# A streaming encoder step on one core: ten pairs for eleven between retrievals, longer runs for the activations, 112 down tiles in three passes

## The reference

```python
m = _mixer(_rmsnorm(x, norm1), ...)        # convolution and retention branches
x = x + m
x = x + _peer(_rmsnorm(x, norm2), wq, sk, u_tab, v_tab)
y = _rmsnorm(x, final_g)

# _peer, for each block of 128 tokens hb
q = (hb @ w_q).reshape(128, 8, 2, 128)
s = einsum('thpd,pkd->thpk', q, sk)                 # 8 heads, 2 sides, 128 keys
sv, si = top_k(s, 16)
cand = sv[:, :, 0, :, None] + sv[:, :, 1, None, :]  # 16 x 16 sums
ts, tp = top_k(cand, 16)                            # 16 experts per head
e = take_along_axis(cidx, tp, -1)                   # numbers in 0..16383
g = softmax(ts)
a = gelu(einsum('thkd,td->thk', u_tab[e], hb))
out = einsum('thkd,thk->td', v_tab[e], g * a)
```

## Time and profile before

| | us |
|---|---|
| median of 3 runs | 2256.77 (2254.47 to 2258.5) |
| the profiled execution | 2255.25 |
| its span, first to last instruction | 2253.4 |
| PE busy | 2175.2 (97%) |
| DVE busy | 1721.3 (76%) |
| POOL busy | 862.4 (38%) |
| ACT busy | 580.5 (26%) |

### The profile page before, as it was taken

One profiled execution on the slowest core, in us unless ns is written; L12 is line 12 of the kernel. 1 busy time (PEld: TensorE's weight loads), 2 busy tenths in 40 slices (PEclk: granted clock), 3 DMA queues, 4 the chain that ended last, 5 costly groups with the idle time before them and its releaser, 6 DMA issues.

```text
span 2253.4 us, 30667 instructions
## 1 busy us (share of the span) xinstructions
PE 2175.2 (97%) x10425; PEld 1683.0 (75%) x10425; DVE 1721.3 (76%) x3228; ACT 580.5 (26%) x1143; POOL 862.4 (38%) x606
## 2 busy tenths in 40 slices
PE   5999999999999999999999999999969999999998
PEld 5988989999998975655565565677737777777774
DVE  3576576676765277988979979999949888888885
ACT  3212223122222111211221211233314333333332
POOL 4322122123342005584684775311244444444430
PEclk9999999999999999999999999999989999999999
DMA  4999889999972459999999999888899999999992
GB/s 163 306 309 315 289 302 310 324 315 312 330 247 108 157 186 365 342 406 412 376 412 412 376 412 413 303 280 279 288 373 395 408 399 385 398 403 383 397 382 82
DMA packets 326439, 735.40 MB, mean 326 GB/s; under 512 B 30368, under 2 KB 179616, under 8 KB 326304
## 3 DMA queue, kind: packets, MB, share of 16 engines
q1 hardware_dynamic: 202080, 439.67, 54.5%
q0 software_dynamic: 73728, 268.47, 30.5%
q10 hardware_dynamic: 50496, 25.59, 3.8%
HBM read 604.04 MB, written 129.57 MB: 326 GB/s over the span
## 4 chain that ended last, share of the span: by engine, by line
PE 57%; DVE 14%; issue 13%; POOL 8%; DMA 7%; SPq 1%; ACT 1%; ACTq 0%; POOLq 0%; DVEq 0%
PE ps L1804 6%; PE ps L1805 6%; PE ps L1806 6%; PE ps L1751 6%; PE ps L1711 6%; PE ps L1812 5%; POOL b L680 5%; PE ps L1517 4%; PE ps L1516 4%; PE ps L1515 4%; PE ps L1766 3%; DVE b L1393 3%; DMA b<-in_peer_v,b 3%; POOL b L645 2%; DMA b<-in_u_t 2%
## 5 line engine op out<-in xcount | busy, mean ns | idle before, releaser
L1751 PE MATMUL ps<-b,b 128*128 128x384 f32 x2048 | 667.0, 487 | 0.0
L680 POOL DMA_INDIRECT b<-u_rows,b x256 | 363.9, 1421 | 743.3 <-DVE b L1376 543.4
L1751 PEld LDWEIGHTS ps<-b,b 128*128 128x128 f32 x2048 | 387.6, 190 | 264.1 <-issue 1.2
L645 POOL TENSOR_TENSOR b<-b,b 128x1024 fp32r<-128x1024 f32 x80 | 196.3, 2457 | 465.1 <-ACT b L693 460.6
L1515 PE MATMUL ps<-b,b 128*128 128x320 f32 x1152 | 364.5, 316 | 1.6 <-issue 1.6
L1393 DVE SCALAR_TENSOR_TENSOR b<-b,b,b 128x1024 f32<-128x1024 f32 x256 | 331.1, 1293 | 34.9 <-issue 16.9
L1517 PE MATMUL ps<-b,b 128*128 128x320 f32 x1152 | 357.1, 310 | 0.0
L1516 PE MATMUL ps<-b,b 128*128 128x320 f32 x1152 | 357.0, 310 | 0.0
L1376 DVE CUSTOM_DVE_ANT_0 b<-b,b 128x1024 f32<-128x1024 f32 x256 | 312.7, 1222 | 30.4 <-DMA b<-u_rows,b 24.4
L680 POOL DMA_INDIRECT b<-in_peer_v,b x256 | 289.3, 1130 | 91.5 <-issue 77.6
L1033 DVE STREAM_TRANSPOSE b<-b 128x1024 f32<-128x1024 f32 x128 | 157.6, 1240 | 166.2 <-DMA b<-in_u_t 161.3
(11 more groups left out here) (164 smaller groups left out, 2656.9 us busy)
## 6 DMA issues: line engine op xcount, KB each, us to landing
b<-in_u_t SPq DMA_DIRECT2D x256, 512.0 KB, 5.7
u_rows<-b SPq DMA_DIRECT2D x512, 128.0 KB, 4.2
b<-in_peer_v SPq DMA_DIRECT2D x128, 512.0 KB
b<-in_w_in SPq DMA_DIRECT2D x72, 512.0 KB
b<-in_wq SPq DMA_DIRECT2D x48, 512.0 KB
acts<-b SPq DMA_DIRECT2D x128, 192.0 KB
gates<-b ACTq DMA_DIRECT2D x12, 2048.0 KB
b<-gates SPq DMA_DIRECT2D x32, 768.0 KB
```

The costliest lines, as they stand in the source:

```text
L645: nc.gpsimd.tensor_tensor(lo[u][:, :], raw[:, u, :], hi[u][:, :].bitcast(F32), ALU.subtract).then_inc(lo_ready, 1)
L680: nc.gpsimd.indirect_dma_start(slots[n % SLOTS][:, :], None, u_rows if kind == "u" else v_rows, bass.IndirectOffsetOnAxis(ap=row_id[:, r_ ...
L1751: last = nc.tensor.matmul(ps[:, e % 4, 0:TD], w[:, k * P:(k + 1) * P], h2[:, k, SD:T], start=(k == 0), stop=(k == KT - 1))
```

## The change

In the order of the diff:

- `BEFORE_DOWNS` goes from five to six and `GAP` from eleven to ten. So each of three gaps has one pair less, one more stands before the downs, and 48 pairs instead of 46 are left for the down stage. `EXP_AT`, `SCORES_AT`, `PICKT_AT` and `GATE_AT` move up by one, two and three up products for the second, third and fourth retrieval with gaps before them; the scatters run in up products 96 to 119, and eight up products follow them instead of five. The slope of `pair_at` is 27.6.
- `three(e)` is true for seven of eight tiles, 112 in all, and no longer excludes the last four; there the tiles 124 to 126 are done in three passes, with the waits for their parts before the first token tile. `down_three` can end a sum.
- `acts` in memory is laid out by group, partition, tile: a group's load has one run of 6 KB for a partition instead of four of 1.5 KB. The stores stay one tile each.
- `fin_y`, `junk` and `fin_g` move onto the buffers of gates and activations (`al`, `gr`), and the load of `final_g` waits for the last product with gates alone.

```diff
--- before.py
+++ after.py
@@ -58,19 +58,19 @@
 BESIDE = 2
 AHEAD = 2
 BESIDE_HOTS = 8
-BEFORE_DOWNS = 5
+BEFORE_DOWNS = 6
 LINES = 4
 EXP_FIRST = -13
-EXP_AT = {1: 7, 2: 36, 3: 64, 4: 93}
-SCORES_AT = {2: 6, 3: 45, 4: 73}
-PICKT_AT = {2: 41, 3: 69, 4: 98}
-GATE_AT = 99
+EXP_AT = {1: 7, 2: 35, 3: 62, 4: 90}
+SCORES_AT = {2: 6, 3: 44, 4: 71}
+PICKT_AT = {2: 40, 3: 67, 4: 95}
+GATE_AT = 96
 GATE_ENDS = GATE_AT + TD // (2 * BLK)
 INSIDE = 9
 RETRIEVAL_AT = -7.6
 DOWN_RING = 2 * GROUP
 HALVES = 4
-GAP = 11
+GAP = 10
 CYCLE = INSIDE + GAP
 HOTS = 4
 EARLY = 4
@@ -89,7 +89,7 @@
         i = b - NPAIR_R
         return GATE_AT + 3 * i if i < BESIDE_HOTS else GATE_ENDS - 2 + i - BESIDE_HOTS
     turn, i = b // CYCLE, b % CYCLE
-    e = RETRIEVAL_AT + 28.6 * turn + (0.5 + 2.0 * i if i < INSIDE else 17.3 + 0.97 * (i - INSIDE))
+    e = RETRIEVAL_AT + 27.6 * turn + (0.5 + 2.0 * i if i < INSIDE else 17.3 + 0.97 * (i - INSIDE))
     return math.floor(e)
 
 
@@ -99,7 +99,7 @@
 
 def three(e):
 
-    return e < NKEY - GROUP and e % 6 != 5
+    return e % 8 != 7
 
 
 THREES = [e for e in range(NKEY) if three(e)]
@@ -339,25 +339,25 @@
 
 
         e = [z_from]
+        f = [z_from]
         al = take(e, [P, 2, GROUP, TD], F32)
         gr = take(e, [P, 2, NB, GROUP, GT], F32)
         p32 = take(e, [P, GROUP, TD], F32)
         p_hi = take(e, [P, GROUP, TD], F32R)
         p_lo = take(e, [P, GROUP, TD], F32R)
-        f = [e[0]]
         v_hi = [take(e, [P, D], F32R) for _ in range(HALVES)]
         v_lo = [take(e, [P, D], F32R) for _ in range(HALVES - 1)] + [at(h_from + 16384, [P, D], F32R)]
         v_more = [at(h_from + 4096 * i, [P, D], F32) for i in range(GROUP)]
         fin_y = take(f, [P, 2, D], F32)
         junk = take(f, [P, D], F32)
         fin_g = take(f, [P, D], F32)
-        assert f[0] <= e[0]
+        assert f[0] <= z_from + 16 * GROUP * TD
         assert e[0] <= top - 16384
 
         ps = ctx.enter_context(nc.psum_tensor("ps", [P, 8, 512], F32))
 
         gates = nc.dram_tensor("gates", [NE_GROUPS, P, NB, GROUP * GT], F32).ap()
-        acts = nc.dram_tensor("acts", [NKEY, P, TD], F32).ap()
+        acts = nc.dram_tensor("acts", [NE_GROUPS, P, GROUP, TD], F32).ap()
 
 
         loaded = [sem(f"raw_loaded{u}") for u in range(GROUP)]
@@ -580,7 +580,7 @@
 
             def acts_out(e):
                 sp.wait_ge(evac, A_U + e + 1)
-                sp.dma_start(tile_of(acts, e), spill[:, e % 2, :]).then_inc(a_stored[e % 2], 16)
+                sp.dma_start(acts[e // GROUP, :, e % GROUP, :], spill[:, e % 2, :]).then_inc(a_stored[e % 2], 16)
 
             for i in range(3 * A_WQ):
                 plain_in(i, io["wq"][i % A_WQ, :, :])
@@ -598,8 +598,8 @@
                     sp.wait_ge(a_stored[i], 16 * (GROUP // 2) * (g + 1))
                 src = gates[g, :, :, :]
                 sp.dma_start(gr[:, g % 2, :, :, :].rearrange("p b k t -> p b (k t)"), src).then_inc(g_loaded[g % 2], 16)
-                src = acts[g * GROUP:(g + 1) * GROUP, :, :].rearrange("k p t -> p k t")
-                sp.dma_start(al[:, g % 2, :, :], src).then_inc(al_loaded[g % 2], 16)
+                src = acts[g, :, :, :].rearrange("p k t -> p (k t)")
+                sp.dma_start(al[:, g % 2, :, :].rearrange("p k t -> p (k t)"), src).then_inc(al_loaded[g % 2], 16)
 
             def down_in(e):
                 if e < GROUP:
@@ -626,8 +626,7 @@
                     for u in range(GROUP):
                         down_in((g + 1) * GROUP + u)
 
-            sp.wait_ge(a_used, A_V + NKEY - GROUP)
-            sp.wait_ge(row_done, ROWS)
+            sp.wait_ge(p_ready, NKEY)
             sp.dma_start(fin_g[:, :], io["final_g"]).then_inc(fin_loaded, 16)
             for tt in range(TT):
                 sp.wait_ge(y_ready, tt + 1)
@@ -1796,6 +1795,10 @@
                 pe.wait_ge(v_loaded[e % DOWN_RING], 16 * (e // DOWN_RING + 1))
                 pe.wait_ge(p_ready, e + 1)
 
+            def split_in(e):
+                pe.wait_ge(v_split, SPLIT[e] + 1)
+                pe.wait_ge(p_split, SPLIT[e] + 1)
+
             def down_three(e, i):
                 u, n = e % GROUP, SPLIT[e] % HALVES
                 tok = slice(i * P, (i + 1) * P)
@@ -1803,7 +1806,7 @@
                     out, cols = ps[:, 2 + 2 * i + dh, :], slice(dh * 512, (dh + 1) * 512)
                     nc.tensor.matmul(out, p_hi[:, u, tok], v_hi[n][:, cols], start=(e == 0), stop=False)
                     nc.tensor.matmul(out, p_hi[:, u, tok], v_lo[n][:, cols], start=False, stop=False)
-                    last = nc.tensor.matmul(out, p_lo[:, u, tok], v_hi[n][:, cols], start=False, stop=False)
+                    last = nc.tensor.matmul(out, p_lo[:, u, tok], v_hi[n][:, cols], start=False, stop=(e == NKEY - 1))
                 return last
 
             def down(e, i):
@@ -1816,8 +1819,7 @@
             for e in range(NKEY - GROUP):
                 down_tile_in(e)
                 if three(e):
-                    pe.wait_ge(v_split, SPLIT[e] + 1)
-                    pe.wait_ge(p_split, SPLIT[e] + 1)
+                    split_in(e)
                 for i in range(ND):
                     last = down_three(e, i) if three(e) else down(e, i)
                 last.then_inc(a_used, 1)
@@ -1825,7 +1827,9 @@
                 for e in range(NKEY - GROUP, NKEY):
                     if i == 0:
                         down_tile_in(e)
-                    last = down(e, i)
+                    if i == 0 and three(e):
+                        split_in(e)
+                    last = down_three(e, i) if three(e) else down(e, i)
                 last.then_inc(sums_done, 1)
```

## The result

The changed kernel takes 2234.2 us (median of 4 runs, 2232.64 to 2235.69) where the kernel before takes 2255.62 beside it; the ratio is 0.9903, 95% interval 0.9889 to 0.9916, so 21.9 us less. The forecast was 2235.6 against 2256.77, 21.2 less. The profiled execution has a span of 2232.5 us; 2232.2 was forecast.

A forecast was written before the change was run, and what follows sets the result against it. PE, busy 2175 of 2253 us, was taken as the bound, with gaps bound by DMA. Gains of 7.7 + 5.1 + 8.4 = 21.2 us gave a span of 2232.2, or 2235.6 us in median terms; range 2225 to 2248.

The forecast's parts named there:

- A pair costs what DMA makes it cost, 23.2 us for three: Gaps between retrievals: dropping each gap's last pair frees DVE of 9.2, 7.15 and 6.85 us, DMA waiting included.
- the second rival: Up stage: a dropped pair saves only DVE's 4.7 us, the stage loses 1.3, total 2244.6 us; chance 0.13.
- The up stage, 7.7 us: Up products to end of scatters: pick waits nearly vanish, 0.2 us left, so the stage ends 7.7 us sooner.
- A gate write of 46 us, a gap of 17.4, 5.1 us: Before the downs: extra traffic lengthens the last gate write, yet PE's gap falls from 22.45 to 17.4, gaining 5.1 us.
- the first rival: Before the downs: the gate write is not prolonged, the gap falls to 7.0, total 2225 us; chance 0.17.
- My estimate from it, some 46 us: Last gate write: alternating its 512-byte runs with 4 KB gathers would keep it some 46 us if traffic lasts.
- Runs of 6 KB, nothing: Group loads of activations: 128 longer runs instead of 512 are worth zero, under 1 us at most.
- Eight tiles more in three passes, 8.4 us: Down products: eight more tiles at 4.10 us instead of 5.15 save 8.4 us if PE stays the bound.
- DVE's cover: Down stage: DVE's extra splits and pairs cost nothing, 38 us of its waiting for PE stays.
- DMA as the narrow cover: Down stage: tiles ask 403 GB/s against a seen ceiling of 410; costs nothing, with 2% of cover.
- The tail, nothing: After the last product: up to 1 us could appear, taken as zero; tail unchanged at 10 us.
- the third and fourth rivals: Down stage short of DMA: at 395 GB/s 2246 us, chance 0.10; at 380 GB/s 2268 us, chance 0.04.

The follow-up runs named there:

- moves_alone: Changed kernel's moved order constants and slope, but gaps of eleven pairs and five pairs before the downs again; ratio 0.9972, span 2244.2 us.
- bd0: Changed kernel with no pair between the scatters and the downs instead of six, 54 in the down stage; ratio 0.9912, span 2232.1 us.
- gap9: Changed kernel taken one step further: gaps of nine pairs, nine pairs before the downs, scatters from up product 93; ratio 0.9928, span 2232.0 us.
- acts_rows: Changed kernel with activations in memory as before, loaded in runs of 1.5 KB; ratio 0.9924, span 2237.4 us.
- threes_back: Changed kernel with 104 down tiles in three passes again, every sixth and the last four in plain fp32; ratio 0.9948, span 2240.9 us.
- bd4: Changed kernel with four pairs before the downs instead of six, 50 in the down stage; ratio 0.9885, span 2220.1 us.
- sp_order: Changed kernel with three more down tiles and activation writes ahead of the first group's load in SP's queue; ratio 0.9939, span 2241.9 us.

## Why the prediction was right, step by step

The sum was 21.2 us off the span, and 20.9 came. That it is so close is partly luck: the stages that the change touches gave 6.0 + 5.4 + 8.5 = 19.9, and 1.05 came from an earlier start of the up products. By its terms, in the profiles of the two kernels:

- *A pair costs what DMA makes it cost, 23.2 us for three.* Right: 22.6 us at the third retrieval, 21.5 counted from the first up product. 14.1, the second rival's price, is out.
- *The up stage, 7.7 us.* 6.0: from the first up product to the end of the scatters it went from 742.2 to 720.7, of which three products sooner are 15.5. The waits for picks stayed at 2.2 us instead of 0.2: at the third pick PE arrived 23.0 us sooner and not 22.1, DVE 22.6 and not 23.2. In absolute time the scatters ended at 1620.4, 22.6 sooner, as if the term had been 7.1; but 1.05 of this lies ahead of the up products and is chance. moves_alone shows that the moves pay nothing without the pairs. That the pairs need the moves is not shown: by the prediction's own working the waits of the picks would go with the pairs alone, and the moves are what shortens the gap; that kernel was not run.
- *A gate write of 46 us, a gap of 17.4, 5.1 us.* 45.6, 17.1 and 5.4. The choice was made against the optimistic end (a gap of 7.0, the first rival), and here the reading of full engines decided it. The plain sum of bytes, some 5 us for each 2.1 MB beside the write, holds while the gathers run dry before the write ends. "2.1 MB that need 5 us alone" were 7.2 us from issue to last packet in bd0. The Trainium skill's taking of turns, packet by packet, as cited in the prediction (DMA: Bandwidth & Descriptors, Queues, rings and completion order), is borne out by the packets of the queues, 659 of the write beside 657 of the gathers. My estimate from it, some 46 us, left out SP's queue and fails at gap9's 60.3; that it came near the measured 45.6 is luck.
- *Runs of 6 KB, nothing.* Borne out by road and down stage of acts_rows, in the profile; the interval of its runs is wider than the claim.
- *Eight tiles more in three passes, 8.4 us.* 8.5 between the two kernels and 8.4 in threes_back, both up to the end of the span. Up to the end of the last product it is 7.6 (552.0 to 544.4), and 0.9 lies in the tail. The products alone fell short because the stretch at half the clock behind the gap held 13 products instead of 7, at 0.2 us each. DVE's cover was worked out as 38 us left; the waits for PE that remain are 46.3.
- *DMA as the narrow cover.* 403 GB/s asked, 410 seen as the ceiling. It held, with windows of 49 to 92 us at 400 to 414. The true edge is 414: bd4 stands on it without loss, bd0 beyond it.
- *The tail, nothing.* DVE's last sums no longer wait for PE, and begin within 0.1 us of its end, though the load of final_g, 4.6 us, has come into the chain. From the last product to the end it is 9.1 us instead of 10.0; why is open.

So the third and fourth rivals, a down stage short of bytes, did not come. The nearest to them is bd0, which asks for more than the ceiling gives: their kind of sum, 1.80 MB at 414 GB/s for a tile against 4.23 us, gives 15 us there, and 9.2 came.

## What to carry to other kernels

When a wait ends on a transfer, ask what else the DMA engines carry until it lands: while they are full, each byte that is moved beside it delays it at the full rate, up to the time that its own turns take, and starting it sooner among more traffic gives that back (gap9 started the write 18 us sooner, won one in the profile and none in the runs). Short packets make a transfer weak among long ones: 512 bytes beside 4 KB got a twelfth of the bytes. And before you read a queue's release as a landing, see what else that queue had before it (bd0). Fill the stage that has PE as its bound with the DMA work up to the measured ceiling, and no further, and keep it away from the transfer that PE waits for. A step moved in one engine's order pays only as far as the engines that feed it come sooner too.

## What the hardware showed that I had not expected

Loads, stores and gathers together ran at 413 to 414 GB/s for 400 us on end in bd4, above the 358 that the Trainium skill (DMA: Bandwidth & Descriptors, section Bandwidth) gives as a core's limit from HBM. The same section says that 358 is what each core gets when both of a domain stream, and has 425 measured for one core alone, and these runs use one core. And an in-order queue cuts both ways: putting three loads and three writes ahead of a blocked load (sp_order) shortened the road by 3.7 us and lengthened by 5.8 the transfer that blocked it.
